# Where the row scales of the next pass are squared, loaded and broadcast in a fused decoder layer: three entries of a schedule moved by half a unit or a unit

## The chip, the cores and the metric

One NeuronCore of one Trainium2 chip runs the whole kernel. The metric is the device time of one execution in microseconds (us); the median of several executions counts. The kernel before ran in 1553.02, 1554.44 and 1556.95 us (median 1554.44 us).

## The reference

One layer of a decoder. A prompt of 2048 tokens (width 1024) and eight single-token samples go through: an RMS norm whose result is scaled and shifted per channel (`h = rms_norm(x) * (1 + scale) + shift`), one input projection that feeds a sliding-window attention and a gated linear recurrence, two output projections `w_proj_a` and `w_proj_b`, a merge of their results by two sigmoid gates (`y = g_a * (ya @ w_proj_a) + g_b * (yb @ w_proj_b)`, the gates being projections of `h`), a last projection `w_out`, and a gated residual.

```
mod = c @ w_ada + b_ada;  shift, scale, gate = split(mod)
h = rms_norm(x, norm_g) * (1 + scale) + shift
proj = h @ w_in                      # q, k, v, za | qb, fb, ib, zb
...
g_a, g_b = split(sigmoid(h @ w_merge + b_merge))
y = g_a * (ya @ w_proj_a) + g_b * (yb @ w_proj_b)
out = x + gate * (y @ w_out)
```

The change touches only the work on the RMS norm of the next stretch of tokens: the sum of squares of each row of `x`, its reciprocal root, and the product of that with `x`.

## The kernel before

The prompt is worked in NIT = 4 passes of 512 tokens. A pass is a list of NU = 68 **units** (`UNITS`), each one accumulation in one of two PSUM banks: unit u writes bank D(u % 2). The units are, in order: 0 to 3 the projections B, 4 to 7 A, 8 to 11 za, 12 to 15 f, 16 to 19 qb, 20 to 23 ib, 24 to 27 zb, then `_merges()`: the gates ga and gb and the output projections pa and pb (among them unit 38 pa0, 39 pb0, 40 pa1, 41 pb1, 42 pa2, 43 pb2, 44 ga5, 45 gb5, 46 pa3, 47 pb3, 48 ga6, 49 gb6, 50 pa4, 51 pb4, 52 pa5, 53 pb5, 54 ga7, 55 gb7, 56 to 59 pa6, pb6, pa7, pb7), and last 60 to 67 the output projection o0, o1. A unit has two halves of equal work on TensorE. Every product of two f32 numbers is made of three matmuls of the parts hi and lo of weights and activations.

Everything that is not such a unit is a **side task**, put by `put(it, u, half, task, a, bank)` behind half `half` of unit `u`. This table is the same for all engines: TensorE (`dense`, `side`), ScalarE (`evac`, then weight splits, then `side`), VectorE (`evac` in the second half of a unit, then `side`) and GpSimd walk through it in the same order, each issuing its own share, and engines wait for each other by semaphores. So the table fixes the order of the work on each engine, and a semaphore can only make an engine wait. A PSUM bank is given back by whoever reads it: TensorE begins a unit on D1 only when the last unit on D1 was read (`s.wait_ge(f"D{u % 2}_free", ...)`, L773 in `dense`).

The tasks that the change touches, in passes 0, 1 and 2 (the last pass has no next one):

- `xst` t: ScalarE squares x tile t of the next pass (128 rows) in two instructions of 512 columns with a running sum (`squares`, L1028), after it has waited for the load of the tile and, because the squares themselves are thrown into a buffer that the gate of unit 41 uses, for VectorE to have read unit 41 (pb1). Tiles 2 and 3 come first, then 0 and 1, since all four share two buffers.
- SyncE's event `x01` loads tiles 0 and 1 into those buffers. It waits until tiles 2 and 3 have been squared (`xst` at 8 + 8 it + 4). Events stand in one queue with the weight loads (L524 issues them all): before the load of weight block n, all events are issued whose unit is at most the unit at which block n - 3 is split.
- `rstd`: VectorE makes the four row scales from the sums of squares in a chain of 17 small instructions (`row_scales`, L1277 to L1280), each settled before the next. It stands at (50, second half), behind VectorE's reading of unit 50 (pa4) and ahead of its reading of unit 51 (pb4, L1438).
- `bc`: TensorE broadcasts the row scales into bank XA by four matmuls (L820, which the trace shows as eight records). It waits for `rstd`.
- `xm` n: VectorE scales and shifts two of the eight blocks of the next x (L1287, L1293), from (54, second half) on. It waits for `bc`.

The weight blocks (128 x 1024) go through three raw buffers: load (L524), the hi part by ScalarE (L1023), the lo part by GpSimd (L1757). In passes 0 and 1 TensorE also uses the raw block once for the eight samples (`bu`, L857 and L863).

Of the kernel before, what the change touches and what calls it, by code (L numbers as in the profile page):

```python
# [98 lines left out]
for _n in reversed(range(NIT * NB)):  # L99
    _t = BEGIN[NU * (_n // NB) + FIRST_UNIT[_n % NB]] - 7  # L100
# [41 lines left out]
def put(it, u, hf, task, a, bank=None, key=None):  # L142

    SIDE.setdefault((it, u, hf), []).append((task, a, bank, key or (it, task, a)))
# [10 lines left out]
def at_half(it, n, *rest):  # L155

    put(it, n // 2, n % 2, *rest)
# [3 lines left out]
for it in range(NIT):  # L161
    if it == 0:
        put(0, 3, 0, "gm", 0, "XA")
        put(0, 4, 1, "late", 0)
        put(0, 8, 0, "gb", 0, "XB")
        put(0, 8, 1, "gS", 0, "XC")
        put(0, 30, 0, "srow", 0)
    if it < 2:
        for _n, _g in enumerate(GROUPS[it]):
            for _b in _g:  # L170
                _s = BURST_AT[it * NB + _b] - it * NU
                if it * NB + _b in PAIR.values():
                    continue
                put(it, int(_s), int(2 * _s) % 2, "bu", _b, "XD", (it, "sg", _n))
            SAMPLE_SLOT[(it, _n)] = _s
    put(it, 2 if it else 20, 0, "at0", 0)
    for _t in range(NT):
        put(it, 2 + _t, 0, "qtB", _t, "XB" if _t % 2 else "XA")
        put(it, 6 + _t, 0, "qtA", _t, "XB" if _t % 2 else "XA")
    put(it, 3, 1, "rsk", 0)  # L180
    put(it, 5, 1, "kt", 0, "XA")
    put(it, 7, 1, "rsq", 0)
    for _n in range(8):
        at_half(it, S_AT[_n], "S", _n, None if _n in AHEAD[it] else "XA")
        at_half(it, S_AT[_n] + 1, "norm", _n)
    for _t in range(NT):
        at_half(it, PV_AT[_t], "PVa", _t, "XA")
        at_half(it, PV_AT[_t], "PV", _t, "XB")
        if _t < 3:
            at_half(it, PV_AT[_t], "turn", 2 * _t + 2)  # L190
    for _n in AHEAD[it]:
        at_half(it, AHEAD_AT[_n], "scores", _n, "XC", (it, "S", _n))
    if it == 0:
        put(0, 20, 0, "dg", 3, "XA", (0, "dg", 0))
    else:
        for _h in range(HB):
            at_half(it, (38, 38, 38, 40)[_h], "dg", _h, "XC", (it, "dg", 0))
    for _l in range(7):
        at_half(it, 42 + 2 * _l, "level", _l, "XA" if _l % 2 else "XB")
    for _t in range(NT):  # L200
        if _t // 2 not in KEYS_TURNED:
            put(it, 28 + _t, 0, "KT", _t, "XC")
        at_half(it, O_AT[_t], "o", _t, "XB")
        at_half(it, O_AT[_t], "st", _t, "XA")
    for _r in KEYS_TURNED:
        at_half(it, 56, "kD", _r)
    for _r in range(2):
        at_half(it, ON_AT[_r], "onorm", _r)
    for _t in range(NT):
        at_half(it, YD_AT[_t], "yD", _t)  # L210
        at_half(it, YT_AT[_t], "yT", _t)
    if it < NIT - 1:
        for _n, _t in enumerate((2, 3, 0, 1)):
            put(it, (42, 43, 46, 47)[_n], 1, "xst", _t)
        put(it, 50, 1, "rstd", 0)
        put(it, 52, 1, "bc", 0, "XA")
        for _n in range(4):
            put(it, (54, 56, 59, 60)[_n], 1, "xm", _n)
            put(it, (57, 58, 61, 62)[_n], 1, "hh", _n)
    if it == 0:  # L220
        for _n in range(11):
            _s = SAMPLE_SLOT[(0, _n)] + 1
            put(0, int(_s), int(2 * _s) % 2, "sy" if _n in (0, 1, 5) else "sx", _n, "XC")
        put(0, 33, 0, "sQ", 0, "XC")
        for _r in range(2):
            _u = (44, 52)[_r]
            put(0, _u, 0, "sT", _r, "XC"), put(0, _u + 1, 1, "sS", _r, "XC"), put(0, _u + 3, 0, "snorm", _r)
            put(0, _u + 4, 1, "sP", _r, "XC"), put(0, _u + 6, 0, "sO", _r, "XC")
    if it == 1:
        for _b in range(NS):  # L230
            put(1, _b + 1, 0, "vB", _b, "XD")
            put(1, _b + 2, 0, "so", _b, "XC", (1, "so", 0))
        put(1, 10, 1, "srms", 0)
        put(1, 13, 0, "soss", 0, "XC")
        for _n in range(6):
            _s = SAMPLE_SLOT[(1, _n)] + 1
            put(1, int(_s), int(2 * _s) % 2, "sx", _n, "XC")
            if _n >= 4:
                _s += 1 + (_n == 4)
                put(1, int(_s), int(2 * _s) % 2, "sOT", _n - 4, "XC")  # L240
# [91 lines left out]
def build(nc, A, O):  # L332

    ctx = ExitStack()
    with ctx:
# [109 lines left out]
        def small(n, start=[0]):  # L445
            a = sm[:, start[0]:start[0] + n]
            start[0] += n
            return a
# [5 lines left out]
        xst, rst, xw1, xw2, xw3 = small(8), small(4), small(4), small(4), small(4)  # L454
# [22 lines left out]
        XA, XB, XC, XD = (pb[b] for b in ("XA", "XB", "XC", "XD"))  # L477
# [42 lines left out]
        def _(sp):  # L520
# [35 lines left out]
            later = {}  # L556
            for it in range(NIT):
                b0 = it * NU
                if it < NIT - 1:
                    later.setdefault(b0 + 33, []).append(("xst", it, 0))  # L560
                    later.setdefault(b0 + 44, []).append(("x01", it, 0))
                    later.setdefault(b0 + 48, []).append(("xh", it, 0))
                    later.setdefault(b0 + (50 if it else 59), []).append(("xh", it, 1))
                later.setdefault(b0 + 5, []).append(("vr", it, 0))
                for r in range(2):
                    if r in KEYS_TURNED:
                        later.setdefault(b0 + KS_AT[r], []).append(("ks", it, r))
                        later.setdefault(b0 + KL_AT[r], []).append(("kl", it, r))
                    later.setdefault(b0 + OS_AT[r], []).append(("os", it, r))
                    later.setdefault(b0 + OL_AT[r], []).append(("ol", it, r))  # L570
                later.setdefault(b0 + 59, []).append(("xr", it, 0))
                for t in range(NT):
                    if it == NIT - 1:
                        later.setdefault(b0 + 60 + t, []).append(("out1", it, t))
                    later.setdefault(b0 + 64 + t, []).append(("out", it, t))
# [140 lines left out]
        def _(pe):  # L716
# [289 lines left out]
            for it in range(NIT):  # L1006
                for u in range(NU):
                    for hf_ in (0, 1):
                        dense(it, u, hf_)
                        for task, a, _, key in SIDE.get((it, u, hf_), []):  # L1010
                            side(it, task, a, key)
# [216 lines left out]
        def _(dve):  # L1228
# [244 lines left out]
            def side(it, task, a, key):  # L1473
# [24 lines left out]
                elif task == "level":  # L1498
# [3 lines left out]
                    fl, fr = blocks(ff, w)  # L1502
                    kl, _ = blocks(kk, w)
                    _, qr = blocks(qq, w)
                    s.done(tt(qr, qr, fl[:, :, :, 0:1].broadcast_to(shape), ALU.mult))  # L1505
                    s.done(tt(kl, kl, fr[:, :, :, 0:1].broadcast_to(shape), ALU.mult))
# [397 lines left out]
```

How the kernel before makes its waits and increments, by code:

```python
    def wait_ge(self, name, n):  # L289
        if n > self.seen.get(name, 0):
            self.e.wait_ge(self.sems[name], n)
            self.seen[name] = n
# [8 lines left out]
    def settle(self):  # L302
        self.wait_ge(*self.at)
# [1 line left out]
    def unit_full(self, it, u):  # L306
        self.wait_ge(f"D{u % 2}_full", (it * NU + u) // 2 + 1)
# [1 line left out]
    def unit_left(self, it, kind, j):  # L310
        u = UIX[(kind, j)]
        self.wait_ge(f"D{u % 2}_free", (it * NU + u) // 2 + 1)
# [5 lines left out]
    def full(self, *key):  # L319
        self.wait_ge(f"{BANK[key]}_full", USE[key] + 1)
# [1 line left out]
    def freed(self, *key):  # L323
        self.wait_ge(f"{BANK[key]}_free", USE[key] + 1)
# [219 lines left out]
            def weights(n):  # L545
                if n >= NRAW:
                    s.wait_ge("w_lo", n - NRAW + 1)
                    if n - NRAW in bursts:
                        s.wait_ge(*bursts[n - NRAW])
                for dst, src in block_dmas(n):
                    load(dst, src, f"w_in{n % NRAW}")
# [34 lines left out]
            def event(what, it, a):  # L586
                half = slice(256 * a, 256 * a + 256)
                if what == "ks":
                    s.wait_ge("kD", len(KEYS_TURNED) * it + KEYS_TURNED.index(a) + 1)
                    s.wait_ge(f"kt_in{a}", 64 * it)
                    load(zk[a].rearrange("i q (h t) j p -> (i q) h (t j p)", t=2), kk[:, :, half], f"kz{a}")
                elif what == "kl":
                    s.wait_ge(f"kz{a}", 16 * (it + 1))
                    for j in range(4):
```

## Time and profile before

| | |
|---|---|
| median of three runs | 1554.44 us (1553.02 to 1556.95) |
| the profiled execution | 1554.78 us, of which 1552.7 us are its span |
| granted TensorE clock, mean | 0.996 |
| TensorE busy | 1516.0 us, 98% of the span |
| GpSimd busy | 831.5 us, 54% |
| VectorE busy | 803.8 us, 52% |
| ScalarE busy | 535.0 us, 34% |
| DMA queue of all loads | 37.0% of 16 engines |

The span is what lies between the first and the last recorded instruction; the execution's own time is 2.08 us more. Busy time of TensorE counts overlapping matmuls once. The places that the change touches are the late parts of passes 0, 1 and 2 (near 325 to 377, 709 to 757 and 1080 to 1123 us).

### The profile page before, as it was taken

To read this page: it belongs to the slowest core of one execution; us is meant where nothing else is said; L and a number is where in the kernel's file an instruction comes from. 1 tells how busy PE (TensorE), PEld (TensorE's weight loads), DVE (VectorE), ACT (ScalarE), POOL (GpSimd) and SP (SyncE) were. 2 spreads that over 40 slices of the span, in tenths; PEclk is the share of its full clock that TensorE was granted. 3 is DMA by queue.
4 is the path that set the end of the run, shared out by engine and by line. 5 is a ranking of instruction groups with operands and counts; after the bars stand their busy time and mean duration, and the time that the engine had idled before them with its cause. 6 is when DMAs were issued, how large, how long until landed. Compare 5 with 4: busy or idle time off the path is not lost.

```text
span 1552.7 us, 31555 instructions
## 1 busy us (share of the span) xinstructions
PE 1516.0 (98%) x12936; PEld 1233.5 (79%) x12936; DVE 803.8 (52%) x1972; ACT 535.0 (34%) x1111; POOL 831.5 (54%) x1074
## 2 busy tenths in 40 slices
PE   5999999999999999999999999999999999999998
PEld 2777778777888777888779878888788977788886
DVE  5767466225558856422444774642253775642122
ACT  4334322434312531344331452243432352243330
POOL 1525433567863643367683472447696363436671
PEclk9999999999999999999999999999999999999999
DMA  9612212534563321443343231244544231244351
GB/s 346 236 55 83 83 57 82 171 117 165 172 202 110 104 69 57 129 143 136 110 164 136 90 122 43 87 120 148 190 165 147 76 110 56 70 123 123 108 169 58
DMA packets 119047, 191.52 MB, mean 123 GB/s; under 512 B 57198, under 2 KB 74951, under 8 KB 118120
## 3 DMA queue, kind: packets, MB, share of 16 engines
q1 hardware_dynamic: 118904, 189.52, 37.0%
q8 instruction: 102, 1.67, 0.4%
q14 instruction: 41, 0.34, 0.1%
HBM read 169.13 MB, written 18.25 MB: 121 GB/s over the span
## 4 chain that ended last, share of the span: by engine, by line
PE 92%; DVE 5%; issue 1%; ACT 1%; DMA 0%; SPq 0%; DVEq 0%
PE ps_D L801 54%; PE ps_D L798 25%; PE ps_XCD L863 1%; PE ps_XB L939 1%; PE ps_XA L964 1%; PE ps_XA L975 1%; PE ps_XA L1001 1%; PE ps_XB L992 1%; PE ps_XB L991 1%; PE ps_XA L939 1%; PE ps_XB L975 1%; DMA s_st_lo<-in_x_prompt 0%; DVE sm L1254 0%; PE ps_XCD L964 0%; DVE sm L1257 0%
## 5 line engine op out<-in xcount | busy, mean ns | idle before, releaser
L1757 POOL TENSOR_TENSOR w_lo_t<-w_raw,w_hi_t 128x256 fp32r<-128x256 f32 x920 | 687.2, 780 | 582.4 <-ACT w_hi_t L1023 582.1
L801 PE MATMUL ps_D<-h_hi_t,w_hi_t 128*128 128x512 f32 x1024 | 409.1, 399 | 0.0
L801 PE MATMUL ps_D<-h_lo_t,w_hi_t 128*128 128x512 f32 x1024 | 399.4, 390 | 0.0
L801 PE MATMUL ps_D<-h_hi_t,w_lo_t 128*128 128x512 f32 x1024 | 399.3, 390 | 0.0
L1023 ACT ACTIVATE w_hi_t<-w_raw 128x1024 fp32r<-128x1024 f32 x232 | 239.9, 1051 | 112.9 <-PE ps_D L798 61.0
L801 PEld LDWEIGHTS ps_D<-h_hi_t,w_hi_t 128*128 128x128 f32 x1024 | 192.2, 188 | 48.0 <-issue 10.0
L801 PEld LDWEIGHTS ps_D<-h_hi_t,w_lo_t 128*128 128x128 f32 x1024 | 192.2, 188 | 41.3
L801 PEld LDWEIGHTS ps_D<-h_lo_t,w_hi_t 128*128 128x128 f32 x1024 | 192.5, 188 | 37.0
L798 PE MATMUL ps_D<-w_hi_t,h_hi_t 128*128 128x384 f32 (+1 forms) x384 | 141.7, 369 | 1.1 <-DVE yf_t L1391 1.0
L798 PE MATMUL ps_D<-w_lo_t,h_hi_t 128*128 128x384 f32 (+1 forms) x384 | 136.7, 356 | 0.0
L798 PE MATMUL ps_D<-w_hi_t,h_lo_t 128*128 128x384 f32 (+1 forms) x384 | 136.4, 355 | 0.0
L798 PE MATMUL ps_D<-w_hi_t,y_hi_t 128*128 128x512 f32 x256 | 100.2, 391 | 1.7 <-issue 1.7
L798 PE MATMUL ps_D<-w_lo_t,y_hi_t 128*128 128x512 f32 x256 | 99.6, 389 | 0.0
L798 PE MATMUL ps_D<-w_hi_t,y_lo_t 128*128 128x512 f32 x256 | 99.6, 389 | 0.0
L798 PEld LDWEIGHTS ps_D<-w_hi_t,h_hi_t 128*128 128x128 f32 x384 | 72.7, 189 | 12.0 <-issue 5.4
L1443 DVE TENSOR_TENSOR acc_or_kst<-ps_D,gate_bc 128x512 f32<-128x512 f32 x32 | 22.1, 692 | 107.4 <-PE ps_D L798 107.3
L1505 DVE TENSOR_TENSOR qq<-qq,ff 128x1024 f32<-128x1024 f32 x28 | 40.6, 1449 | 70.7 <-PE ps_XB L939 46.8
L798 PEld LDWEIGHTS ps_D<-w_lo_t,h_hi_t 128*128 128x128 f32 x384 | 72.7, 189 | 5.3
L1168 ACT ACTIVATE p_or_hf<-p_or_hf,sm 128x160 f32<-128x160 f32 x128 | 53.3, 419 | 67.3 <-DVE sm L1552 65.9
L798 PEld LDWEIGHTS ps_D<-w_hi_t,h_lo_t 128*128 128x128 f32 x384 | 72.8, 190 | 4.7
L1092 ACT ACTIVATE th_t<-ps_D,bm_half 128x512 f32<-128x512 f32 x40 | 27.6, 690 | 128.5 <-PE ps_D L801 128.5
L1594 DVE SCALAR_TENSOR_TENSOR state<-state,ff,ps_XA 128x128 f32<-128x128 f32 x64 | 18.0, 344 | 79.2 <-PE ps_XA L1001 79.2
(389 smaller groups left out, 2323.1 us busy)
## 6 DMA issues: line engine op xcount, KB each, us to landing
w_raw<-in_w_blocks SPq DMA_DIRECT2D x232, 512.0 KB, 3.4
xr<-in_x_prompt SPq DMA_DIRECT2D x16, 512.0 KB, 5.2
x_or_AT<-in_x_prompt SPq DMA_DIRECT2D x14, 512.0 KB, 5.4
out_dram<-xr SPq DMA_DIRECT2D x12, 512.0 KB, 2.9
z_o<-kk SPq DMA_DIRECT2D x8, 512.0 KB, 3.1
x_or_AT<-in_x_turned SPq DMA_DIRECT2D x3, 1024.0 KB, 6.0
p_or_hf<-in_x_turned SPq DMA_DIRECT2D x3, 1024.0 KB, 5.6
z_k<-kk SPq DMA_DIRECT2D x4, 512.0 KB, 4.7
```

What stands on the lines that cost most here:

```text
L798: ins = mm(bank[:, 0:P * nb].rearrange("p (n c) -> p n c", c=P), a[:, k, P * j:P * j + P], w[:, s0:s0 + nb, k, :], start=go, stop=end)
L801: ins = mm(bank[:, :], w[:, s0, k0 + k, :], a[:, k, :], start=go, stop=end)
L863: ins = mm(dst, hS[:, k, :], raw[:, :, k, :], start=k < 4, stop=k >= 4)
L939: ins = mm(bank[row:row + left, m * col:m * col + m], kk[:, h, c + 32 * g:c + 32 * g + left], right, start=True, stop=True)
L975: ins = mm(dst[DH * g:DH * g + DH], val[:, DH * g:DH * g + DH], PT[r, g, :, 32 * j:32 * j + 32], start=j == 0, stop=j == 4)
L1023: s.done(fn(w_hi[:, SLOT[n % NB]], w_raw[:, n % NRAW], ACT.Copy), "w_hi")
L1092: s.leave(fn(dst, bank[:, :], ACT.Tanh, scale=0.5, bias=bm_half[:, c:c + 1]), it, u)
L1168: fn(p_t[:, m, :], p_t[:, m, :], ACT.Exp, bias=negm[:, m:m + 1], accum_out=rsum[:, m:m + 1])
L1443: leave(tt(acc[:, 0:w], bank[:, 0:w], gate_bc[:, c0:c0 + w], ALU.mult), it, u)
L1505: s.done(tt(qr, qr, fl[:, :, :, 0:1].broadcast_to(shape), ALU.mult))
L1594: ins = stt(state[:, h, :], state[:, h, :], ff[:, h, P * a:P * a + 1], bank[:, P * h:P * h + P], ALU.mult, ALU.add)
L1757: ins = g_.tensor_tensor(w_lo[:, c, k:k + 2], w_raw[:, n % NRAW, k:k + 2], f32(w_hi[:, c, k:k + 2]), ALU.subtract)
```

## The change

Three numbers of the table are changed. The squares of x tiles 2 and 3 go from the second halves of units 42 and 43 to those of units 41 and 42; the squares of tiles 0 and 1 stay where they are. The event that loads tiles 0 and 1 goes from unit 44 to unit 43. The broadcast of the row scales goes from behind the second half of unit 52 to behind the first half of unit 53. The making of the row scales stays at (50, second half).

```
-            put(it, (42, 43, 46, 47)[_n], 1, "xst", _t)
+            put(it, (41, 42, 46, 47)[_n], 1, "xst", _t)
         put(it, 50, 1, "rstd", 0)
-        put(it, 52, 1, "bc", 0, "XA")
+        put(it, 53, 0, "bc", 0, "XA")
...
-                    later.setdefault(b0 + 44, []).append(("x01", it, 0))
+                    later.setdefault(b0 + 43, []).append(("x01", it, 0))
```

In pass 1 the place (53, first half) already holds a `bu`, which stands ahead of the broadcast there.

## Rows read from the trace of the kernel before

**Rows 1.** The page: busy time by engine; shares of the chain that ended last.

```profile
PE 1516.0 (98%) x12936; PEld 1233.5 (79%) x12936; DVE 803.8 (52%) x1972; ACT 535.0 (34%) x1111; POOL 831.5 (54%) x1074
...
PE 92%; DVE 5%; issue 1%; ACT 1%; DMA 0%; SPq 0%; DVEq 0%
```

**Rows 2.** Waits of TensorE over the span: us in total, times, longest us.

```profile
PE ps_XA L820 <- DVE sm L1280: 2.8, 2, 1.6
```

**Rows 3.** Timeline of TensorE, pass 1: start us, us, what, count [idle, releaser].

```profile
751.65 0.39 PE L801 MATMUL ps_D<-w_hi_t,w_lo_t 128*128 128x512 f32 x1
753.30 1.13 PE L820 MATMUL ps_XA<-ident,sm 128*128 128x128 f32 x8 [1.27 <-DVE sm L1280]
754.19 0.49 PE L801 MATMUL ps_D<-yb_hi_t,w_hi_t 128*128 128x512 f32 x1
...
755.76 1.07 PE L857 MATMUL ps_XCD<-w_raw,cT_or_ab 128*32 128x256 f32 x16
```

**Rows 4.** Timeline of TensorE, the same place in pass 2.

```profile
1120.78 1.13 PE L820 MATMUL ps_XA<-ident,sm 128*128 128x128 f32 x8 [1.56 <-DVE sm L1280]
1121.66 0.48 PE L801 MATMUL ps_D<-yb_hi_t,w_hi_t 128*128 128x512 f32 x1
```

**Rows 5.** Timeline of TensorE, the same place in pass 0.

```profile
376.03 1.05 PE L820 MATMUL ps_XA<-ident,sm 128*128 128x128 f32 x8
376.84 0.48 PE L801 MATMUL ps_D<-yb_hi_t,w_hi_t 128*128 128x512 f32 x1
377.16 0.39 PE L801 MATMUL ps_D<-yb_lo_t,w_hi_t 128*128 128x512 f32 x1
```

**Rows 6.** Timeline of VectorE, pass 1, from unit 50's reading to unit 51's.

```profile
746.70 0.69 DVE L1425 SCALAR_TENSOR_TENSOR acc_or_kst<-ff,ps_D 128x512 f32<-128x512 f32 x1 [2.05 <-PE ps_D L801]
747.42 0.56 DVE L1277 TENSOR_TENSOR sm<-sm 128x4 f32<-128x4 f32 x1
...
750.11 0.66 DVE L1254 TENSOR_TENSOR sm<-sm 128x4 f32<-128x4 f32 x1
750.80 0.16 DVE L1255 TENSOR_TENSOR sm<-sm 128x4 f32<-128x4 f32 x1
...
753.19 0.69 DVE L1438 SCALAR_TENSOR_TENSOR yf_t<-ff,ps_D 128x512 f32<-128x512 f32 x1
```

**Rows 7.** Timeline of VectorE, pass 2: unit 51's reading and the first `xm`.

```profile
1120.66 0.69 DVE L1438 SCALAR_TENSOR_TENSOR yf_t<-ff,ps_D 128x512 f32<-128x512 f32 x1
...
1126.80 0.75 DVE L1287 SCALAR_TENSOR_TENSOR x_or_AT<-x_or_AT,gscale,ps_XA 128x512 f32<-128x512 f32 x1
```

**Rows 8.** Timeline of VectorE, pass 0: unit 51's reading.

```profile
374.12 0.69 DVE L1438 SCALAR_TENSOR_TENSOR yf_t<-ff,ps_D 128x512 f32<-128x512 f32 x1
```

**Rows 9.** Timeline of GpSimd, pass 1: weight splits.

```profile
745.13 5.62 POOL L1757 TENSOR_TENSOR w_lo_t<-w_raw,w_hi_t 128x256 fp32r<-128x256 f32 x8 [3.88 <-ACT w_hi_t L1023]
...
781.28 3.23 POOL L1757 TENSOR_TENSOR w_lo_t<-w_raw,w_hi_t 128x256 fp32r<-128x256 f32 x4 [1.98 <-ACT w_hi_t L1023]
```

**Rows 10.** Timeline of VectorE, pass 1: unit 41's reading.

```profile
708.24 0.69 DVE L1438 SCALAR_TENSOR_TENSOR yf_t<-p_or_hf,ps_D 128x512 f32<-128x512 f32 x1 [2.02 <-PE ps_D L801]
```

**Rows 11.** Timeline of ScalarE, pass 1: around the squares.

```profile
709.74 0.63 ACT L1114 ACTIVATE y_hi_t<-yf_t 128x512 fp32r<-128x512 f32 x1 [3.80 <-DVE yf_t L1439]
710.27 0.62 ACT L1028 ACTIVATE p_or_hf<-x_or_AT 128x512 f32<-128x512 f32 x1
...
731.91 0.18 ACT L1028 ACTIVATION_READ_ACCUMULATOR p_or_hf<-x_or_AT 128x1 f32 x1
```

**Rows 12.** Timeline of SyncE's queue: the loads of tiles 0 and 1, passes 0 to 2.

```profile
337.42 0.91 SPq L524 DMA_DIRECT2D x_or_AT<-in_x_prompt  x2
...
714.08 0.81 SPq L524 DMA_DIRECT2D x_or_AT<-in_x_prompt  x2
...
1086.86 0.91 SPq L524 DMA_DIRECT2D x_or_AT<-in_x_prompt  x2
```

**Rows 13.** Timeline of TensorE, pass 1: its longest idle stretch behind the change.

```profile
784.61 0.47 PE L798 MATMUL ps_D<-w_hi_t,y_hi_t 128*128 128x512 f32 x1 [1.68 <-issue]
```

## The prediction

> **What bounds the kernel now.** I read the busy times and the chain of the page first, then the waits of TensorE, and then the timelines of each engine around the three places. TensorE is busy for 98% of the span and holds 92% of the chain that ended last [rows 1]. So a change pays only by TensorE's idle time, or costs by adding to it. The reader is to see in its waits that the broadcast `bc` is one of the few places that idle at all: 2.8 us in two stretches, both ended by the last instruction of the row scales (L1280) [rows 2]. They lie in pass 1 (1.27 us before 753.30) [rows 3] and in pass 2 (1.56 us before 1120.78) [rows 4]; in pass 0 the broadcast starts without a wait [rows 5].
>
> **What VectorE does there.** In pass 1 it reads unit 50 from 746.70 to 747.39, makes the row scales from 747.42 to about 753.16 in 17 settled instructions, and only then, at 753.19, reads unit 51 (L1438), until 753.88 [rows 6]. Unit 51 lies in bank D1, and so does unit 53, so TensorE may not begin unit 53 before 753.88. That is the second wait at this place, hidden today: TensorE waits for the scales, broadcasts from 753.30, and when it comes to unit 53 at 754.19 [rows 3] D1 has been free for 0.31 us. The broadcast fills time in which unit 53 could not have started anyway.
>
> **Part 1, the broadcast behind half of unit 53.** It removes no matmul and adds none. TensorE now reaches the wait for D1 first. How fast it reacts: the broadcast began 0.11 us after VectorE had gone on to L1438 (753.19 to 753.30), and VectorE leaves 0.03 us between instructions (747.39 to 747.42) [rows 3, 6], so 0.14 us from an end on VectorE to a start on TensorE. Unit 53 then starts at 753.88 + 0.14 = 754.02, which is 0.17 us earlier than 754.19. Behind its first half comes the broadcast, now with nothing to hide in, at its full price from start to the next start: 0.89 us in pass 1 (753.30 to 754.19) [rows 3]. Net for pass 1: 0.89 - 0.17 = +0.72 us. In pass 2 the reading of unit 51 ends at 1120.66 + 0.69 = 1121.35 [rows 7], unit 53 starts at 1121.49 instead of 1121.66, and the broadcast costs 1121.66 - 1120.78 = 0.88 us [rows 4]: +0.71 us. In pass 0 the reading ends at 374.12 + 0.69 = 374.81 [rows 8], 1.22 us before TensorE has finished unit 52 at 376.03 [rows 5]; neither place waits, and the broadcast costs its 0.81 us (376.03 to 376.84) in either: 0.
>
> Bounds. The inline broadcast isn't seen in the new place. Its nearest price from below is 0.81 us [rows 5], from above the whole duration of the group, 1.13 us [rows 3]; I take 0.89, since the clock and the matmuls are those of rows 3. What the earlier start gives back lies between 0 (TensorE is slower to react) and 0.31 us (it starts at the very end of the reading). Each of passes 1 and 2 so costs 0.50 to 1.13 us. In pass 1 the broadcast comes right behind the burst L857, which interrupts unit 53 at the same place today [rows 3], so two interruptions become one; that may give back some 0.1 us and stays in the bounds. The readers of the broadcast lose nothing: the first `xm` of pass 2 starts at 1126.80, when VectorE is done with its own queue [rows 7], and the broadcast now ends near 1121.49 + 1.5 for the half unit + 1.13 = 1124.1.
>
> Is the delay given back later? The longest idle stretch of TensorE behind this place is 1.68 us before 784.61 [rows 13]. It ends with the split of a weight block on GpSimd at 781.28 + 3.23 = 784.51 [rows 9]. That block's load waits for a burst of TensorE at unit 57, so it moves with TensorE, and the stretch stays as long. I take full carry; if the load came on its own time, pass 1 would cost nothing and the whole change 0.71 us.
>
> **Part 2, the squares one unit earlier.** They are four instructions and their four accumulator reads per pass (8 squares in all are made; half of them move), on ScalarE, 34% busy. The new place waits for VectorE's reading of unit 41, in pass 1 over at 708.24 + 0.69 = 708.93 [rows 10]. The copy of pb1's result to its hi part stands behind it and starts now at 709.74 [rows 11]. Two squares with their reads take 1.5 us (twice about 0.75: 0.62 and a read of 0.18, nearly end to end [rows 11]), so that copy starts at about 710.4, 0.7 us late; the consumer is the output projection in unit 60 and, for its buffer, the reading of unit 47. The squares of tile 3 move ahead of a weight split for unit 46, which slips by under 1 us, far ahead of its use. Nothing gets earlier on TensorE: the row scales don't wait for squares. The last square, which isn't moved, ends at 732.09, and the scales start at 747.42, 15.3 us later, behind the reading of unit 50 [rows 11, 6]. Cost 0, bounds 0 to +0.7 us should the late copy be awaited after all; no gain, because the table leaves `rstd` where it was.
>
> **Part 3, the x load.** Per pass two DMAs of 512 KB. SyncE takes them when the block split at unit 43 stands three loads back. Working that through the list of splits, they come one weight load earlier in passes 0 and 2 and at the same place of the queue in pass 1, where the split at 44 is the first to pass either limit. They go out at 337.42, 714.08 and 1086.86 now [rows 12]; in pass 1 they will go as soon as tile 3 is squared, some 1.5 us earlier (one pair of squares and reads), and in passes 0 and 2 ahead of a weight load instead of behind it. Behind them stands the weight load of pa4 (unit 50), which itself waits for GpSimd's split of pa3. Cost 0: their readers, the squares of tiles 0 and 1, keep their places from unit 46 on.
>
> **A rule of the chip.** The row scales have two speeds: the five instructions from 747.42 to 750.80 take 0.68 us each, the twelve from 750.80 to 753.19 0.20 us each [rows 6], and the change comes where GpSimd's split ends, at 745.13 + 5.62 = 750.75 [rows 9]. The Trainium skill, page "SBUF — State Buffer", section "SBUF: two separate sides", states that VectorE and GpSimd take a shared pair of ports as an exclusive lock held for a whole instruction; by that rule the trace agrees, and the scales would be fast if the split weren't beside them. The sum would be another only if the change parted the two, which is the first rival.
>
> **The sum.** 0 + 0.72 + 0.71 = +1.43 us. On the profiled execution's own 1554.78 us (span 1552.7 and 2.08 outside it) that makes 1556.2 us. The median of the runs shown is 0.34 us lower, 1554.44; I forecast 1554.44 + 1.43 = 1555.9 us. Its own bounds, +0.7 to +2.3 us, are 1555.1 to 1556.7 us, to which the spread of the runs comes (1553.02 to 1556.95).
>
> **Rivals.**
>
> *The wait goes.* If VectorE had read unit 51 by the time TensorE ends unit 52 (at 753.30 - 1.27 = 752.03), the half unit would cover the rest of the scales, and the 2.8 us of rows 2 would vanish: 1551.6 us. For it: that is the only wait on the scales. It decides from 1.9 us: the reading must be over 753.88 - 752.03 earlier. Earlier squares can't do it (15.3 us of slack). A split of GpSimd off the scales could: five instructions at 0.20 instead of 0.68 us save 2.4 us. But that split is released by ScalarE's copies in the queue for unit 49, which nothing in the change moves. Chance 0.10.
>
> *A weight block comes late.* SyncE stops at the x load until tile 3 is squared, with the load of pa4 behind it in passes 0 and 2, and 1 MB goes ahead of it. Seen price of a late block: 1.68 us [rows 13], twice, on top of mine: 1559.2 us. Against: the squares end before the split of pa3 that pa4's load waits for anyway. It decides when the squares of tile 3 end later than pa4's load goes out today, just ahead of the x load at 337.42 and 1086.86 [rows 12]. Chance 0.06.
>
> *Pass 1 is absorbed* in the stretch before 784.61: +0.71, 1555.2 us. Chance 0.08.
>
> **How the numbers follow.** My own forecast holds 0.76. The range 1552.8 to 1558.6 takes in it and the absorbed case with the spread of runs, and leaves out most of the first two rivals. About 0.3% (4.7 us) is what a measurement of this kernel can tell from no change; every case but the late block lies inside it. Faster 0.02 (noise on the first rival), slower 0.05, same 0.93.
>
> **What would show it.** Right: in passes 1 and 2 an idle stretch of about 1.9 us on TensorE before the first matmul of unit 53 (752.03 to 754.02), ended by VectorE's reading L1438 instead of L1280, and L820 with no wait half a unit later; L1277 starting right behind the reading of unit 50 as before; the first squares at the end of L1438 of unit 41; no new wait at unit 46 or 50. Wrong: no idle stretch before unit 53, or one of the same total as before; a wait of TensorE for L1757 in units 44 to 52; a total idle time of TensorE that falls.

## The result and the profile after

The changed kernel ran in 1558.54 us (median of 22 runs, 1554.87 to 1562.36), the kernel before beside it in 1554.76 us (22 runs, 1552.58 to 1558.33). The ratio is 1.0022, with a 95% interval of 1.0015 to 1.0029: slower by 3.8 us in the medians, by 3.4 us (2.3 to 4.5) by the ratio. That is under the 0.3% named in the prediction but clear of zero. The forecast was 1.4 us slower, 1555.9 us. Way and mechanism hold; the size was too small by a factor of 2.6.

The page of the changed kernel, busy times:

```profile
span 1556.4 us, 31555 instructions
PE 1515.6 (97%) x12936; PEld 1233.7 (79%) x12936; DVE 809.6 (52%) x1972; ACT 535.4 (34%) x1111; POOL 829.3 (53%) x1074
```

TensorE's work is the same (1515.6 against 1516.0 us in [rows 1]), so the 3.7 us of span by which it is longer (1556.4 against 1552.7) lie in waits and in stretches where the work goes on at a slower pace. The waits of TensorE in the changed kernel (us in total, times, longest), where [rows 2] stood before:

```profile
PE ps_D L801 <- DVE yf_t L1438: 4.1, 2, 2.2
...
PE ps_D L798 <- issue: 2.1, 1, 2.1
...
PE ps_XCD L882 <- DVE smS L1457: 1.4, 1, 1.4
```

The wait of 2.8 us on the row scales (L1280) is gone from the list, and one of 4.1 us on VectorE's reading of unit 51 (L1438) has taken its place. TensorE in pass 1, to be read beside [rows 3]:

```profile
752.47 0.39 PE L801 MATMUL ps_D<-w_hi_t,w_lo_t 128*128 128x512 f32 x1
754.76 0.50 PE L801 MATMUL ps_D<-yb_hi_t,w_hi_t 128*128 128x512 f32 x1 [1.91 <-DVE yf_t L1438]
...
756.36 1.07 PE L857 MATMUL ps_XCD<-w_raw,cT_or_ab 128*32 128x256 f32 x16
757.36 1.16 PE L820 MATMUL ps_XA<-ident,sm 128*128 128x128 f32 x8
758.27 0.48 PE L801 MATMUL ps_D<-yb_hi_t,w_hi_t 128*128 128x512 f32 x1
...
759.75 0.40 PE L801 MATMUL ps_D<-h_hi_t,w_hi_t 128*128 128x512 f32 x1
```

This is the forecast picture: idle for 1.91 us, half of unit 53, the burst, and then the broadcast in the open, 0.91 us from start to next start (757.36 to 758.27). From the last matmul of unit 52 to the first of unit 54 it is 7.28 us (752.47 to 759.75). Before it was 6.60, from 751.65 in [rows 3] to this one:

```profile
758.25 0.39 PE L801 MATMUL ps_D<-h_hi_t,w_hi_t 128*128 128x512 f32 x1
```

So +0.68 us, where the prediction had +0.72. Pass 2 of the changed kernel, beside [rows 4], is another matter:

```profile
1120.62 0.39 PE L801 MATMUL ps_D<-w_hi_t,w_lo_t 128*128 128x512 f32 x1
1123.19 0.79 PE L801 MATMUL ps_D<-yb_hi_t,w_hi_t 128*128 128x512 f32 x1 [2.17 <-DVE yf_t L1438]
1123.78 0.63 PE L801 MATMUL ps_D<-yb_lo_t,w_hi_t 128*128 128x512 f32 x1
1124.20 0.63 PE L801 MATMUL ps_D<-yb_hi_t,w_lo_t 128*128 128x512 f32 x1
...
1125.91 1.28 PE L820 MATMUL ps_XA<-ident,sm 128*128 128x128 f32 x8
1126.95 0.48 PE L801 MATMUL ps_D<-yb_hi_t,w_hi_t 128*128 128x512 f32 x1
...
1128.42 0.39 PE L801 MATMUL ps_D<-h_hi_t,w_hi_t 128*128 128x512 f32 x1
```

The idle stretch is 2.17 us (the prediction's terms make it 2.3), but the matmuls behind it last 0.63 us instead of 0.39 and follow each other at 0.43 us instead of 0.23. Busy time by stretches (us, then busy time of each engine and, third from the end, the granted TensorE clock) shows why:

```profile
1119.00:1121.00 2.00, 2.00 (x9) 1.32 (x8) 1.83 (x6) 0.00 (x0) 1.21 (x2) 1.00 0.95 381
1123.00:1126.30 3.30, 3.11 (x8) 2.54 (x9) 1.51 (x3) 2.41 (x3) 1.70 (x2) 0.50 0.31 125
1126.30:1129.00 2.70, 2.70 (x17) 2.35 (x16) 0.32 (x1) 0.43 (x2) 2.70 (x5) 0.99 0.00 0
```

From 1123.0 on the clock was granted at 0.50, its 1.2 GHz level, for 3.3 us, after an idle stretch; then it is back at 2.4 GHz. In the kernel before, the same work ran at full clock throughout:

```profile
1120.80:1124.10 3.30, 3.30 (x19) 2.88 (x20) 1.93 (x3) 1.99 (x3) 1.28 (x2) 1.00 0.43 174
```

In pass 0 the way from the middle of unit 52 (L882) to unit 54's first matmul takes 6.58 us (374.33 to 380.91) where it took 6.60 (374.14 to 380.74), so the forecast of nothing holds there. From unit 52's last matmul to unit 54's first, pass 2 took 7.80 us (1120.62 to 1128.42) against 5.66 before (1118.83 to 1124.49): +2.14 us for a forecast of +0.71. The two places make 2.8 of the 3.7 us of span. The rest is spread over other idle stretches: those near 571 and 599 us are 0.7 us longer together (0.95 and 0.67 before, 1.34 and 0.94 now), the one of [rows 13] is 0.5 us longer (1.68 before, 2.14 now), and others give a little back. The last profiles below show that such stretches differ from one execution to the next of one and the same kernel.

The squares cost ScalarE what was worked out. ScalarE in pass 1 of the changed kernel, beside [rows 11]:

```profile
709.83 0.63 ACT L1028 ACTIVATE p_or_hf<-x_or_AT 128x512 f32<-128x512 f32 x1 [3.07 <-issue]
...
711.21 0.62 ACT L1114 ACTIVATE y_hi_t<-yf_t 128x512 fp32r<-128x512 f32 x1
711.73 0.62 ACT L1028 ACTIVATE p_or_hf<-x_or_AT 128x512 f32<-128x512 f32 x1
...
713.10 1.04 ACT L1023 ACTIVATE w_hi_t<-w_raw 128x1024 fp32r<-128x1024 f32 x1
```

Everything in this pass stands about 0.8 us later than before. With that taken off, the copy L1114 starts at 710.4, as forecast (709.74 before), and the split L1023 at 712.3 instead of 711.6. The x load goes out at 333.54, 713.22 and 1084.47 (337.42, 714.08 and 1086.86 in [rows 12]). Nobody on TensorE waits for any of it.

### The profile page after: what moved, and what is told of

It reads as the page before. It is cut to its first block, busy times and chain, and to the rows that moved or that the text cites. A ratio compares the mean times of both kernels' runs of the same rounds, so it can differ in the third digit from the quotient of the medians.

```text
span 1556.4 us, 31555 instructions
## 1 busy us (share of the span) xinstructions
PE 1515.6 (97%) x12936; PEld 1233.7 (79%) x12936; DVE 809.6 (52%) x1972; ACT 535.4 (34%) x1111; POOL 829.3 (53%) x1074
## 4 chain that ended last, share of the span: by engine, by line
PE 91%; DVE 5%; SPq 1%; issue 1%; DMA 1%; ACT 1%; DVEq 0%
PE ps_D L801 54%; PE ps_D L798 25%; PE ps_XCD L863 1%; SPq L524 1%; PE ps_XB L939 1%; PE ps_XA L964 1%; PE ps_XA L975 1%; PE ps_XA L1001 1%; PE ps_XB L992 1%; PE ps_XB L991 1%; PE ps_XA L939 1%; DMA w_raw<-in_w_blocks 1%; PE ps_XB L975 1%; PE ps_XCD L964 0%; PE ps_XCD L874 0%
## 5 line engine op out<-in xcount | busy, mean ns | idle before, releaser
L801 PE MATMUL ps_D<-h_hi_t,w_hi_t 128*128 128x512 f32 x1024 | 409.1, 400 | 0.0
L801 PE MATMUL ps_D<-h_lo_t,w_hi_t 128*128 128x512 f32 x1024 | 399.4, 390 | 0.0
L801 PE MATMUL ps_D<-h_hi_t,w_lo_t 128*128 128x512 f32 x1024 | 399.3, 390 | 0.0
L1023 ACT ACTIVATE w_hi_t<-w_raw 128x1024 fp32r<-128x1024 f32 x232 | 239.9, 1051 | 116.2 <-PE ps_D L798 61.8
L801 PEld LDWEIGHTS ps_D<-h_hi_t,w_hi_t 128*128 128x128 f32 x1024 | 192.3, 188 | 48.0 <-issue 10.0
L801 PEld LDWEIGHTS ps_D<-h_hi_t,w_lo_t 128*128 128x128 f32 x1024 | 192.2, 188 | 41.3
L801 PEld LDWEIGHTS ps_D<-h_lo_t,w_hi_t 128*128 128x128 f32 x1024 | 192.5, 188 | 37.0
```

What stands on the lines that cost most here:

```text
L801: ins = mm(bank[:, :], w[:, s0, k0 + k, :], a[:, k, :], start=go, stop=end)
L1023: s.done(fn(w_hi[:, SLOT[n % NB]], w_raw[:, n % NRAW], ACT.Copy), "w_hi")
```

## The experiments

All times are medians. The ratio is to the kernel before as it ran beside each on the same chip; times of different rows can be from different chips, and the ratio differs from that of two medians by up to 0.1%. Gains and losses in us are of medians unless the text says by the ratio.

| | time, us | ratio (95%) |
|---|---|---|
| changed kernel | 1558.54 | 1.0022 (1.0015 to 1.0029) |
| e1 squares and load alone | 1554.82 | 1.0001 (0.9992 to 1.0010) |
| e2 broadcast alone | 1557.83 | 1.0020 (1.0012 to 1.0029) |
| e3 changed, stretch filled | 1555.34 | 1.0005 (0.9996 to 1.0014) |
| e4 before, scales early | 1549.65 | 0.9973 (0.9962 to 0.9985) |
| e5 changed, scales early | 1550.51 | 0.9971 (0.9961 to 0.9982) |
| e6 broadcast at 52, first half | 1560.42 | 1.0040 (1.0025 to 1.0054) |
| e9 scales early, burst at 57.0 | 1553.54 | 0.9988 (0.9979 to 0.9996) |
| e10 scales early again | 1551.94 | 0.9972 (0.9962 to 0.9983) |

**e1 and e2: which part of the change costs.** One keeps the squares and the load moved and puts the broadcast back, the other moves the broadcast alone.

```
e1:  -        put(it, 53, 0, "bc", 0, "XA")      (in the changed kernel)
     +        put(it, 52, 1, "bc", 0, "XA")
e2:  -        put(it, 52, 1, "bc", 0, "XA")      (in the kernel before)
     +        put(it, 53, 0, "bc", 0, "XA")
```

> Squares of tiles 2 and 3 at units 41 and 42 and the x load at 43, broadcast left behind (52, second half). Theory (only the broadcast costs): no change against the kernel before, ratio 1.000 within 0.001, and TensorE waits 1.3 and 1.6 us for L1280 in passes 1 and 2 as there. Rival (the earlier squares or load cost a part of the 3.8 us): 1 us or more slower, with a new wait of TensorE for a weight split or a bank.

> Only the broadcast moved, behind the first half of unit 53. Theory: the whole change is in it, 3 to 4 us slower than before, ratio 1.002 to 1.0025, like the changed kernel; of that 1.4 us are the broadcast no longer hidden in a wait, and the rest comes from executions in which TensorE's granted clock drops to its lower level after the longer idle stretch before unit 53. Rival (part of the cost lies with squares or load): 1.4 us slower, ratio 1.0009.

Measured 1.0001 and 1.0020: no cost of the squares and the load is seen (the interval leaves room for 1.6 us), and the broadcast alone is as slow as the whole change. In e1 TensorE waits at the broadcast for 1.28 and 1.55 us; in e2 before unit 53 for 1.90 and 2.18 us, and there the lower clock stands behind both. TensorE of e2 in pass 1 and the clock of that stretch:

```profile
754.14 0.50 PE L801 MATMUL ps_D<-yb_hi_t,w_hi_t 128*128 128x512 f32 x1 [1.90 <-DVE yf_t L1438]
756.03 1.94 PE L857 MATMUL ps_XCD<-w_raw,cT_or_ab 128*32 128x256 f32 x16
757.90 1.54 PE L820 MATMUL ps_XA<-ident,sm 128*128 128x128 f32 x8
760.67 0.39 PE L801 MATMUL ps_D<-h_hi_t,w_hi_t 128*128 128x512 f32 x1
```

```profile
755.00:758.50 3.50, 3.50 (x23) 1.53 (x22) 0.54 (x1) 1.89 (x3) 2.94 (x4) 0.54 0.02 5
```

Unit 53 with its burst and broadcast takes 6.53 us here (754.14 to 760.67) and took 4.99 us at full clock in the changed kernel (754.76 to 759.75). A stretch of lower clock so costs 1.5 us.

**e3: the stretch filled.** The changed kernel, with matmuls that nobody reads behind unit 52 in passes 1 and 2.

```
+        if it:
+            put(it, 52, 1, "fill", 0, "XA", (it, "bc", 0))
         put(it, 53, 0, "bc", 0, "XA")
...
+                if task == "fill":
+                    for k in range(5):
+                        mm(bank[:, 0:TB], w_hi[:, SLOT[BIX[("pa", 5)]], k, :], yb_hi[:, k % 4, :], start=True, stop=True)
+                    return
```

> The changed kernel, with five extra matmuls of 512 columns behind unit 52 in passes 1 and 2, whose result is thrown away (they write bank XA before the broadcast does). They fill 1.1 us of the idle stretch and take none of the work's time, since unit 53 waits for VectorE until 1.9 us later anyway. Clock theory: the lower clock isn't seen in the profile, the time falls from 3.8 to about 1.4 us over before (ratio 1.0009), and the spread of the runs narrows. Rival (the clock has no part, the broadcast simply costs 3.8 us): as slow as the changed kernel, 1.0022, or slower by the matmuls.

1.0005, 2.5 us below e2 on the same chip (1557.83 to 1555.34). TensorE of e3 in pass 1 (L803 is the L801 of the others, L1444 the L1438):

```profile
751.59 0.39 PE L803 MATMUL ps_D<-w_hi_t,w_lo_t 128*128 128x512 f32 x1
751.81 1.29 PE L821 MATMUL ps_XA<-yb_hi_t,w_hi_t 128*128 128x512 f32 x5
753.87 0.50 PE L803 MATMUL ps_D<-yb_hi_t,w_hi_t 128*128 128x512 f32 x1 [0.77 <-DVE yf_t L1444]
```

Unit 53 starts 2.28 us behind the last matmul of unit 52, as in the changed kernel (752.47 to 754.76, 2.29 us). In pass 2 the idle time before unit 53 and the clock behind both places are these:

```profile
1124.24 0.50 PE L803 MATMUL ps_D<-yb_hi_t,w_hi_t 128*128 128x512 f32 x1 [1.05 <-DVE yf_t L1444]
```

```profile
753.87:757.27 3.40, 3.40 (x29) 2.28 (x30) 1.36 (x2) 2.25 (x4) 1.98 (x3) 1.00 0.02 5
1124.24:1127.64 3.40, 3.40 (x19) 2.97 (x20) 1.36 (x2) 2.53 (x3) 1.99 (x3) 1.00 0.24 99
```

The extra matmuls neither cost nor give time by their own length. What they change is that 0.77 and, in pass 2, 1.05 us of idle time are left of 1.91 and 2.17, and the clock stays at full speed behind both. So the changed kernel with ten matmuls more is faster than without them. The rival, a broadcast that costs 3.8 us by itself, falls; the +1.4 us by which I had priced the change (1.0009) lie inside the interval of e3. One thing expected of e3 did not come: its runs spread over 4.5 us, no less than the 4.7 us of e2 and not clearly less than the 5.1 us of the kernel before beside it.

**e6: a longer stretch.** The broadcast half a unit the other way.

```
-        put(it, 52, 1, "bc", 0, "XA")
+        put(it, 52, 0, "bc", 0, "XA")
```

> The kernel before with the broadcast moved half a unit the other way, behind the first half of unit 52. TensorE then waits for the scales with half a unit less of work behind it: 2.6 and 2.9 us idle in passes 1 and 2 instead of 1.27 and 1.56. By the waits alone 2 x 1.45 us slower, 1557.6 us, ratio 1.0019. Clock theory: the longer stretches bring the lower clock in both passes, about 1.5 us each for one stretch of 3.4 us at half rate, so 1560 us or more, ratio 1.0035 or more, and the profile shows a granted clock below 0.9 behind at least one of the two. Rival (the lower clock behind these stretches is chance): 1.0019.

```profile
754.53 1.92 PE L820 MATMUL ps_XA<-ident,sm 128*128 128x128 f32 x8 [2.63 <-DVE sm L1280]
756.10 0.77 PE L801 MATMUL ps_D<-w_hi_t 128*128 128x512 f32 x1
756.67 0.63 PE L801 MATMUL ps_D<-w_lo_t,w_hi_t 128*128 128x512 f32 x1
```

1.0040, and both stretches (2.63 and 2.91 us) have the lower clock behind them. The time is 5.2 us over before in the medians, 6.2 by the ratio, against 2.7 by the growth of the two idle stretches and 2.9 by the expectation; that price (1.0019) lies just below the interval of 1.0025 to 1.0054. In pass 0 a wait of 1.21 us on the scales appears too, but it takes the place of the wait of 1.45 us on L1457, and unit 53 starts no later for it. With five runs this is the thinnest of the comparisons.

**e7 and e8: the two kernels once more, one profile each.**

> The changed kernel again, one profile. Theory: idle stretches of 1.9 and 2.2 us before unit 53 in passes 1 and 2, and the lower clock behind none, one or both; the span goes up by about 1.5 us with each.

> The kernel before again, one profile. Theory: stretches of 1.3 and 1.6 us before the broadcast and no lower clock behind them; the stretches near 571, 599, 785, 1303 and 1331 us differ by some tenths from one execution to the next without any change, up to 0.5 us at 785.

Three stretches of the changed kernel in e7, at the first matmul behind each idle stretch:

```profile
752.80:756.20 3.40, 3.38 (x14) 2.12 (x18) 1.37 (x2) 1.58 (x2) 1.97 (x3) 0.52 0.00 0
1124.70:1128.10 3.40, 3.40 (x11) 2.90 (x12) 1.35 (x2) 2.52 (x3) 2.00 (x3) 0.55 0.25 100
786.80:790.20 3.40, 3.40 (x11) 2.62 (x10) 1.06 (x2) 0.00 (x0) 3.40 (x6) 0.54 1.01 407
```

All profiles together, idle time in us and the clock behind it:

| kernel | pass 1, unit 52 or 53 | pass 2, the same | near 785 us |
|---|---|---|---|
| before | 1.27 full | 1.56 full | 1.68 full |
| before, e8 | 1.27 full | 1.56 full | 2.14 lower |
| e1 | 1.28 full | 1.55 full | 0.66 full |
| changed | 1.91 full | 2.17 lower | 2.14 full |
| changed, e7 | 1.90 lower | 2.18 lower | 2.14 lower |
| e2 | 1.90 lower | 2.18 lower | 0.96 full |
| e3 | 0.77 full | 1.05 full | 2.14 lower |
| e6 | 2.63 lower | 2.91 lower | 0.69 full |

With the old place of the broadcast none of six stretches brought the lower clock, with the new one five of six. The same length can go either way: 2.14 us near 785 did and did not. That stretch was 1.68 and 2.14 us in two executions of the kernel before, and 0.66 to 2.14 us over all these kernels, none of which changes anything between unit 54 and that place; so it is one source of the spread.

Six stretches are few. Every run also has its mean granted clock, and one drop of 3.4 us to half takes 0.0011 off it. The mean over the runs is 0.9947 for the changed kernel (22 runs), against 0.9966, 0.9963 and 0.9961 for the three groups of runs of the kernel before: 1.3 to 1.7 drops more in an execution, where five of six would be 1.7. In e6 it is 0.9942 beside 0.9963, 1.9 drops more, and in e1 and e3 0.9967 and 0.9966, none more than in the kernel before beside them (0.9966). In e2 it is 0.9957 beside 0.9966, only 0.8 more. So the drops are there over all runs; how many an execution has lies between 0.8 and 1.9, which the profiles alone don't fix.

**e4, e5: the scales made early.** The row scales, not the broadcast, are what VectorE does too late: they stand between its readings of units 50 and 51.

```
-        put(it, 50, 1, "rstd", 0)
+        put(it, 48, 0, "rstd", 0)
```

> The kernel before with the row scales made at (48, first half) instead of (50, second half); the squares are done by then (732 against 733 us in pass 1). Theory: the chain of 17 instructions then stands ahead of VectorE's idle time, the waits on L1280 go (1.42 and 1.72 us start to start in passes 1 and 2), and in pass 0 the wait of 1.45 us on L1457, which stood behind the scales: 4.5 us faster, about 1550 us, ratio 0.997. Rival (another wait takes their place at unit 52 or 53, such as D1 or the sample's column sums): under 1.5 us faster.

> The changed kernel (broadcast behind half of unit 53) with the row scales made at (48, first half). Theory: the place of the broadcast costs only because unit 53 waits there for VectorE's late reading of unit 51; with the scales made early nothing waits, and the time is that of the kernel before with early scales, 1549.7 us, ratio 0.997. Rival (a broadcast inside a unit is itself dearer than between units): 1 us or more above that, 1550.7 us or more.

VectorE and then TensorE of e4 in pass 1:

```profile
730.84 0.59 DVE L1277 TENSOR_TENSOR sm<-sm 128x4 f32<-128x4 f32 x1
...
739.48 0.17 DVE L1280 TENSOR_SCALAR sm<-sm 128x4 f32<-128x4 f32 x1
...
747.19 0.69 DVE L1438 SCALAR_TENSOR_TENSOR yf_t<-ff,ps_D 128x512 f32<-128x512 f32 x1 [2.02 <-PE ps_D L801]
```

```profile
749.42 0.39 PE L801 MATMUL ps_D<-w_hi_t,w_lo_t 128*128 128x512 f32 x1
749.65 1.05 PE L820 MATMUL ps_XA<-ident,sm 128*128 128x128 f32 x8
750.46 0.48 PE L801 MATMUL ps_D<-yb_hi_t,w_hi_t 128*128 128x512 f32 x1
```

The chain takes longer there (730.84 to 739.65, 8.8 us instead of 5.7), but in time that VectorE had to spare. Its reading of unit 51 now waits for TensorE instead of the other way round, the broadcast follows unit 52 without a gap, and in pass 0 the wait of 1.4 us on L1457 is gone too. 0.9973, and 0.9972 when repeated (e10): by the ratio 4.2 us faster than before. With the scales early no effect of the broadcast's place is seen: e5 has 0.9971, and from unit 52's last matmul to unit 54's first pass 1 takes 5.07 us there (750.04 to 755.11) and 5.10 us in e4 (749.42 to 754.52). So the broadcast's place costs only where VectorE reads unit 51 late, and that lateness is the fault to mend.

**e9 and e10: the stretch near 785.** In pass 1 the load of the fourth block of the output projection waits for a burst of TensorE on the first two; e9 puts this half a unit earlier, on top of e4.

```
-OUT_AT = (56.5, 57.5, 58, 59.5, 60.5, 61, 61.5, 62.5)
+OUT_AT = (56.5, 57, 58, 59.5, 60.5, 61, 61.5, 62.5)
```

> The kernel with early scales, and the sample burst on the first two blocks of the output projection half a unit earlier in pass 1 (57.0 instead of 57.5), since the load of the fourth block waits for it and TensorE then waits for that block's split near 782 us, 2.1 us in the runs so far, with the lower clock behind it. Theory: the split comes 1.4 us earlier, the stretch shrinks from 2.1 to about 0.8 us and the lower clock behind it goes: 1.4 + 1.5 us faster than with early scales alone, 1547 us, ratio 0.995 to the kernel before. Rival (the split is held up by GpSimd's other work): no change, 1549.7 us.

> The kernel with early scales again, beside the one with the earlier burst: 1549.7 us, ratio 0.9973, with 0.7 to 2.1 us of idle time near 781 us, and the lower clock behind it where the stretch is the longer one.

A miss: 0.9988, slower than e10 beside it by 1.6 us in the medians. The waits of TensorE in e9:

```profile
PE ps_D L798 <- POOL y_lo_t L1790: 2.2, 1, 2.2
...
PE ps_D L798 <- issue: 1.0, 1, 1.0
...
PE ps_D L798 <- POOL y_lo_t L1773: 0.4, 1, 0.4
```

The stretch shrinks to 1.0 us and the clock stays full, as hoped. But ScalarE now waits 9.31 us for that block (2.74 us in e10) with two other copies queued behind it, L1039 and L1114, which in e10 were done before that wait (at 769.98 and 776.88). Its timeline in e9:

```profile
778.45 1.06 ACT L1023 ACTIVATE w_hi_t<-w_raw 128x1024 fp32r<-128x1024 f32 x1 [9.31 <-DMA w_raw<-in_w_blocks]
779.41 1.04 ACT L1039 ACTIVATE h_hi_t<-x_or_AT 128x1024 fp32r<-128x1024 f32 x1
780.36 0.61 ACT L1114 ACTIVATE y_hi_t<-yf_t 128x512 fp32r<-128x512 f32 x1
```

GpSimd gets to the results of the merge later (L1790 at 789.91 instead of 787.70 in e10), and TensorE waits 0.4 and 2.2 us for those instead. The best version run is that with the scales early; between e4, e5 and e10 the ratios do not tell.

## Why the prediction was right in its way and short in its size

*The second wait at the place.* Right, and the core of it. That unit 53 waits for D1, that VectorE gives D1 back only behind the scales, and that the broadcast was hidden in this wait, is what the new wait list shows (L1438 for L1280). The idle stretches follow from its terms as 2.0 and 2.3 us (its last paragraph says 1.9) and came out at 1.91 and 2.17; the open broadcast as 0.89 and came out at 0.91; pass 1 as +0.72 and came out at +0.68.

*The bounds of the broadcast.* This is the step that failed: "I take 0.89, since the clock and the matmuls are those of rows 3", and with it its own bounds of +0.7 to +2.3 us. I had the longer idle stretch on paper and priced it by its length alone. What the runs put in its place is a third term: behind the stretches before unit 53 the granted clock fell to 1.2 GHz in five of six, 1.5 us each, which makes 2 x 0.7 + 2 x 5/6 x 1.5 = 3.9 us against 3.8 measured. That the two agree to 0.1 us is partly luck: with the 1.3 to 1.7 drops that the mean clocks give, the sum is 3.4 to 4.0 us, and for e2, with 0.8, it is 2.6 against 3.2 measured. The term itself is shown from two sides: filling the stretch takes 2.5 us back (e3), and lengthening it costs 5.2 us where the waits give 2.7 to 2.9 (e6).

*The range.* The measured 1558.54 us lies within 1552.8 to 1558.6 by 0.06 us. That is luck: the range was drawn for the spread of the runs and not for a term of 2.4 us, and the sum's own bounds end at 1556.7 us.

*Squares and x load at nothing.* Right by e1 alone (1.0001, within 0.0010) and by the rows: the copy behind the squares 0.7 us late and asked for by nobody, the scales not started by the squares but by the reading of unit 50. In passes 0 and 2 the x load stands one weight load earlier, and no wait for a split appears.

*Carried on later.* No sign that the stretch near 785 absorbs the delay: it is 2.14 us in both profiles of the changed kernel, 1.68 and 2.14 in those of the kernel before. But it is 0.96 us in e2 and 0.66 us in e1, so it varies by more than the 0.7 us in question, which one trace could not show.

*The rivals.* The wait did not go, as the slack of 15.3 us said. No block came late. One premise of the first rival was wrong: the waits of [rows 2] are not the only ones on the scales. In pass 0 of the kernel before TensorE waits 1.45 us for L1457, which stands on VectorE right behind the last of the scales (373.59):

```profile
373.80 0.29 DVE L1457 TENSOR_REDUCE smS<-ps_XCD 128x32 f32<-128x128 f32 x1
```

With the scales early that wait goes as well (e4). The two speeds of the scales were weighed as a way to a shorter chain; e4 shows that the chain needn't be shorter, only elsewhere: in pass 1 ten of its instructions ran at the slow speed beside GpSimd's work instead of five, it took 8.8 us instead of 5.7, and the kernel was faster.

## What to carry to other kernels

When an instruction that waits is moved behind other work, look at what that other work waits for: if both hang on the same engine's queue, the move only takes the instruction out of the shadow of the wait and adds its own length. Here the fault lay with the producer, 17 small instructions queued ahead of a bank's reader on VectorE, and moving that was worth 4.2 us by the ratio where moving the consumer lost 3.4. And an idle stretch of TensorE has a second price behind its length, which a trace of the shorter stretch can't show; where one cannot be avoided, matmuls that nobody reads can be cheaper than silence, as they were here (e3).

## What the runs showed of the hardware

The granted clock fell to 0.50 for 3.4 us at single idle stretches of 1.9 to 2.9 us in an otherwise 98% busy TensorE, at a price of 1.5 us each. The drop need not begin with the first matmul behind the stretch: in e2 the matmuls of pass 1 slow down 1.0 us after it (0.40 us each up to 754.95, 0.63 us from 755.47). It is not certain for any one stretch: of those of 1.9 us or more in the table (the eight profiles have no other behind the first 50 us), ten had the lower clock behind them and two had not (1.91 and 2.14 us, both in one execution). Near 785 us e4, e5 and e10 had it behind 2.14, 2.31 and 2.19 us, e9 had a stretch of 2.19 us at 790 us without it, and e10 had it once more behind 1.59 us, near 571 us. With the stretches of 1.3 and 1.6 us at the old place it was not seen in six, and e6 had 1.57 us near 571 without it. Why one stretch brings it and an equal one doesn't stays open.
